# An encoder layer on one core: Fourier position transform split by four, with a three-pass projection

## What is computed

```python
def fourier_mix(f):
    """f: (B,S,FOURIER_WIDTH). Real part of 2-D DFT over (positions, group channels)."""
    B, S, _ = f.shape
    u = f.reshape(B, S, N_FOURIER_GROUPS, FOURIER_GROUP_DIM).astype(jnp.float32)   # 4 groups of 128
    re = jnp.fft.fft2(u, axes=(1, 3), norm="ortho").real
    return re.reshape(B, S, FOURIER_WIDTH).astype(f.dtype)

def encoder_layer(x, ...):
    h = rmsnorm(x, norm1_g)
    q, k, v, f, ga, gf = jnp.split(h @ w_in, SPLITS, axis=-1)
    ...
    o_na = neighborhood_attention(q, k, v, rpb) @ w_na_out
    o_f = fourier_mix(f) @ w_fourier
    x = x + (jax.nn.sigmoid(ga) * o_na + jax.nn.sigmoid(gf) * o_f) @ w_out
    return x + expert_choice_ffn(rmsnorm(x, norm2_g), ...)       # 16 experts
```

## Time and profile before

| | |
|---|---|
| Time, median of 3 runs (lowest to highest) | 2915.61 us (2912.18 to 2917.41) |
| Profiled execution: span from first to last instruction | 2913.2 us |
| Busy: PE, PEld, DVE, ACT, POOL | 91%, 75%, 58%, 42%, 31% |
| Mean granted TensorE clock | 0.956 |
| Tokens, to the first projection | 0 to 32.5 us |
| Fourier, to the last copy to ofT | 32.5 to 245.2 us |

### The profile page before, as it was taken

How to read it: one execution, slowest core, us unless ns; L and a number is a source line. 1 busy time by engine, 2 the same in 40 slices (tenths; PEclk the granted TensorE clock), 3 DMA queues, 4 the chain that set the end, 5 groups by cost and what they waited for, 6 DMA issues and landing times.

```text
span 2913.2 us, 46659 instructions
## 1 busy us (share of the span) xinstructions
PE 2660.3 (91%) x17898; PEld 2197.9 (75%) x17898; DVE 1681.9 (58%) x2075; ACT 1229.0 (42%) x1685; POOL 903.3 (31%) x352
## 2 busy tenths in 40 slices
PE   7999999999999999479989899998999999899997
PEld 4456677676777768368888888888888888888887
DVE  3011422432110143677987887797788779778876
ACT  2011333332000021145665565566566556656554
POOL 0004111110111000234344444434444443443443
PEclk9999999999999999789999999999999999999999
DMA  7211010010110143347787787778778777877872
GB/s 234 40 27 40 17 34 21 6 36 4 40 43 22 29 178 125 144 149 255 266 269 250 258 265 250 258 269 266 249 257 278 250 249 269 268 253 252 287 249 68
DMA packets 340356, 489.78 MB, mean 168 GB/s; under 512 B 22090, under 2 KB 194777, under 8 KB 340192
## 3 DMA queue, kind: packets, MB, share of 16 engines
q1 hardware_dynamic: 332864, 461.60, 46.9%
q0 software_dynamic: 7328, 25.58, 4.1%
HBM read 462.28 MB, written 24.87 MB: 167 GB/s over the span
## 4 chain that ended last, share of the span: by engine, by line
PE 62%; issue 23%; DVE 11%; ACT 2%; DMA 1%; SPq 0%; DVEq 0%; POOL 0%; ACTq 0%; POOLq 0%
PE ps L1267 28%; PE ps L1524 15%; PE ps L1527 7%; PE ps L1447 4%; PE ps L1372 3%; DVE gu L1200 2%; DVE act_f L1207 2%; PE ps L1385 2%; DVE w_lo L434 1%; DVE act_b L1213 1%; DVE act_hl L1215 1%; ACT w_hi L855 1%; PE ps L1514 1%; PE ps L1332 1%; DMA spos_s_sb<-in_spos_s 1%
## 5 line engine op out<-in xcount | busy, mean ns | idle before, releaser
L434 POOL TENSOR_TENSOR w_lo<-raw,w_hi 128x2048 bf16<-128x2048 f32 x132 | 635.5, 4816 | 800.7 <-ACT w_hi L855 800.7
L1524 PE MATMUL ps<-x_hl,w_hi 128*128 128x320 f32 x4112 | 755.9, 327 | 128.4 <-issue 78.3
L855 ACT ACTIVATE w_hi<-raw 128x2048 fp32r<-128x2048 f32 x388 | 739.2, 1906 | 3.0 <-issue 3.0
L1524 PEld LDWEIGHTS ps<-x_hl,w_hi 128*128 128x128 f32 x4112 | 630.2, 195 | 146.0 <-issue 82.6
L434 DVE TENSOR_TENSOR w_lo<-raw,w_hi 128x2048 bf16<-128x2048 f32 x256 | 624.8, 2441 | 96.0 <-ACT w_hi L855 96.0
L1527 PE MATMUL ps<-x_b,w_lo 128*128 128x160 bf16 x4112 | 382.6, 237 | 0.0
L1524 PE MATMUL ps<-act_hl,w_hi 128*128 128x320 f32 x2048 | 349.0, 322 | 0.0
L1527 PEld LDWEIGHTS ps<-x_b,w_lo 128*128 128x128 bf16 x4112 | 279.0, 100 | 54.0 <-issue 3.2
L1524 PEld LDWEIGHTS ps<-act_hl,w_hi 128*128 128x128 f32 x2048 | 311.9, 194 | 2.0
L1207 DVE TENSOR_TENSOR act_f<-silu,gu 128x160 f32<-128x160 f32 x256 | 213.7, 835 | 19.4 <-ACT silu L880 19.4
L873 ACT ACTIVATE lows<-ps 128x320 f32<-128x320 f32 x256 | 111.0, 434 | 254.9 <-PE ps L1527 253.7
(11 more groups left out here) (179 smaller groups left out, 2997.0 us busy)
## 6 DMA issues: line engine op xcount, KB each, us to landing
raw<-in_w_g SPq DMA_DIRECT2D x64, 2048.0 KB, 9.0
raw<-in_w_u SPq DMA_DIRECT2D x64, 2048.0 KB, 11.4
raw<-in_w_d SPq DMA_DIRECT2D x64, 2048.0 KB, 9.1
m_raw<-in_w_in SPq DMA_DIRECT2D x16, 512.0 KB, 4.7
h_raw<-in_w_in SPq DMA_DIRECT2D x12, 512.0 KB, 4.0
x_in<-in_x SPq DMA_DIRECT2D x10, 512.0 KB, 4.2
x_res<-in_x SPq DMA_DIRECT2D x10, 512.0 KB, 4.1
y_out<-x SPq DMA_DIRECT2D x10, 512.0 KB, 2.9
```

Of the source, the lines that this page charges most:

```text
L434: engine.tensor_tensor(unit(w_lo, v), raw_half(v), unit(w_hi, v).bitcast(F32), ALU.subtract)\
L855: act.activation(unit(w_hi, w), raw_half(w), ACT.Copy).then_inc(hi_ready, 1)
L1524: pe.matmul(out, unit(w_hi, v)[:, k, cols], hl[:, k, :, :].rearrange("p a n -> p (a n)"), start=k == 0, stop=False)
```

## The change

**Projection.** The tokens' high and low parts are made tile by tile in the token stage: after each gain ScalarE copies the high part (token_high), GpSimd subtracts for the low one. Each group's weight is split likewise (f_weight_high on ScalarE, then GpSimd), in two buffers, and TensorE projects in three passes, 24 fp32r matmuls for a chunk. The late splits go.

**Positions.** With positions taken modulo four (modulo two for the sample), the transform of 1024 positions becomes four of 256: ScalarE copies tile pairs 0 and 1 (kept), VectorE forms their sums and differences with pairs 2 and 3 in PSUM and then the four turned combinations, TensorE multiplies each by a quarter of the table's rows and columns. The tables are loaded by their first 256 rows (128 for the sample) and regrouped by VectorE, once, so that columns of one remainder lie together. ScalarE writes the result to ofT, at every fourth place (every second for the sample).

**Order.** TensorE runs the channel transform of group g, then the projection of group g+1, then the positions of group g. PSUM banks are assigned anew. The loops over tiles and groups are written out. SP issues the tables without a wait, and each f_w once the one before has been split. GpSimd stores the skewed table and loads the mask after all its token and weight subtractions.

The diff without its memory layout, semaphores and most removed lines:

```diff
+            for u in range(2):
+                sp.dma_start(pos_raw[u][:, :, :], (pos_c, pos_s)[u][0:2 * P, :].rearrange("(k p) n -> p k n", p=P))\
+                  .then_inc(f_tables, 16)
+                sp.dma_start(spos_raw[u][:, :], (spos_c, spos_s)[u][0:P, :]).then_inc(f_tables, 16)
+            for g in range(1, FG):
+                sp.wait_ge(f_w_split, g)
+                f_load(g)
...
+            for t in range(NT):
+                c, first = place_of_tile(t)
+                pool.wait_ge(a_high, t + 1)
+                pool.tensor_tensor(hx_lo[:, :, P * t:P * t + P], hT[:, :, P * t:P * t + P],
+                                   hx_hi[c][:, :, first:first + P].bitcast(F32), ALU.subtract).then_inc(a_split, 1)
+            for g in range(FG):
+                pool.wait_ge(f_w_high, g + 1)
+                pool.tensor_tensor(f_w_lo[g % 2][:, :, :], f_w[:, :, :], f_w_hi[g % 2][:, :, :].bitcast(F32),
+                                   ALU.subtract).then_inc(f_w_split, 1)
             pool.dma_start(skew, rpb_pad[:, :].rearrange("q (o x) -> q o x", o=1)
                            .broadcast_to([HEADS * RPB_H, GRID, SKEW])).then_inc(skew_stored, 16)
             pool.dma_start(mask_sb[:, :], col_mask).then_inc(mask_loaded, 16)
             pool.wait_ge(mask_loaded, 16)
...
+            def token_high(t):
+                c, first = place_of_tile(t)
+                act.wait_ge(a_out, t + 1)
+                act.activation(hx_hi[c][:, :, first:first + P], hT[:, :, P * t:P * t + P], ACT.Copy)\
+                   .then_inc(a_high, 1)
+            def f_weight_high(g):
+                act.wait_ge(f_loaded, 16 * g + 16)
+                if g == 1:
+                    act.wait_ge(a_tr, NT)
+                if g >= 2:
+                    act.wait_ge(f_proj, 3 * (g - 2) + 3)
+                act.activation(f_w_hi[g % 2][:, :, :], f_w[:, :, :], ACT.Copy).then_inc(f_w_high, 1)
+            for t in range(NT):
+                u = t % A_TILES
+                act.wait_ge(a_loaded[u], t // A_TILES * 16 + 16)
+                act.activation(junk_a[:, :], x_in[u][:, :], ACT.Square, accum_out=ss[:, u:u + 1])\
+                   .then_inc(a_stat, 1)
+                inv_rms(a_stat, t * 3, ss[:, u:u + 1], u, D)
+                if t >= 2:
+                    token_high(t - 2)
+            for t in (NT - 2, NT - 1):
+                token_high(t)
+            f_weight_high(0)
+            for g in range(FG):
                 for c, (c0, cn) in enumerate(CHUNKS):
                     act.wait_ge(f_proj, g * 3 + (c + 1))
                     act.activation(fT[:, c0:c0 + cn], bank(c, cn), ACT.Copy).then_inc(f_copied, 1)
+                if g + 1 < FG:
+                    f_weight_high(g + 1)
+                if g:
+                    act.wait_ge(f_mixed, 12 * g)
+                for u in range(2):
+                    act.wait_ge(f_chan, g * 5 + (u + 1))
+                    act.activation(f_kept[u][:, :, :], bank(3 + u).rearrange("p (t n) -> p t n", n=2 * FD),
+                                   ACT.Copy).then_inc(f_copy, 1)
+                act.wait_ge(f_chan, g * 5 + 5)
+                act.activation(fs_kept[:, :], bank(7, 2 * FD), ACT.Copy).then_inc(f_copy, 1)
+                of_s = ofT[:, g, S_PROMPT:TOK].rearrange("p (b a) -> p a b", a=2)
+                of_p = ofT[:, g, 0:S_PROMPT].rearrange("p (b h a) -> p a h b", h=2, a=2)
+                for n, b in enumerate((7, 5, 6)):
+                    act.wait_ge(f_pos, 3 * g + (n + 1))
+                    act.activation(of_p[:, n - 1, :, :] if n else of_s,
+                                   bank(b, BANK if n else S_SAMPLE).rearrange("p (a b) -> p a b", a=2), ACT.Copy)\
+                       .then_inc(f_out, 1)
...
+            def norm(t):
+                u = t % A_TILES
+                dve.wait_ge(a_stat, 3 * t + 3)
+                if t >= 3:
+                    dve.wait_ge(a_tr, t - 2)
+                dve.tensor_scalar(xn_a[t % 3][:, :], x_in[u][:, :], rstd[:, u:u + 1], None, ALU.mult)\
+                   .then_inc(a_norm, 1)
+            def gain(t):
+                dve.wait_ge(a_tr, t + 1)
+                times_gain(hT[:, :, P * t:P * t + P], ps[:, 1024 * (t % 3):1024 * (t % 3) + 1024]
+                           .rearrange("p (k n) -> p k n", n=P), g1_sb[:, :], P).then_inc(a_out, 1)
+            norm(0)
+            for t in range(1, NT):
+                norm(t)
+                gain(t - 1)
+            gain(NT - 1)
+            dve.wait_ge(f_tables, 16 * 4)
+            for u in range(2):
+                dve.tensor_copy(spos_sb[u][:, :, :], spos_raw[u][:, :].rearrange("p (b a) -> p a b", a=2))\
+                   .then_inc(f_regrouped, 1)
+                for n in range(2):
+                    dve.tensor_copy(pos_sb[u][:, n, :, :], pos_raw[u][:, n, :].rearrange("p (b a) -> p a b", a=4))\
+                       .then_inc(f_regrouped, 1)
+            for g in range(FG):
+                done = 12 * g
+                add, sub = ALU.add, ALU.subtract
+                of_bank = [bank(3 + u).rearrange("p (t n) -> p t n", n=2 * FD) for u in range(2)]
+                for u in range(2):
+                    dve.wait_ge(f_copy, 3 * g + (u + 1))
+                    dve.wait_ge(f_chan, 5 * g + (u + 3))
+                    if g:
+                        dve.wait_ge(f_mixed, done)
+                    dve.tensor_tensor(f_sum[u][:, :, :], f_kept[u][:, :, :], of_bank[u], add).then_inc(f_mixed, 1)
+                    dve.tensor_tensor(f_dif[u][:, :, :], f_kept[u][:, :, :], of_bank[u], sub).then_inc(f_mixed, 1)
+                dve.wait_ge(f_copy, 3 * g + 3)
+                if g:
+                    dve.wait_ge(f_pos, 3 * g)
+                for k, op in enumerate((add, sub)):
+                    dve.tensor_tensor(fs_turned[:, k, :], fs_kept[:, :], bank(7, 2 * FD, first=2 * FD), op)\
                        .then_inc(f_mixed, 1)
+                dve.wait_ge(f_mixed, done + 4)
+                for k, op in ((0, add), (2, sub)):
+                    dve.tensor_tensor(f_turned[:, k, :, :], f_sum[0][:, :, :], f_sum[1][:, :, :], op)\
+                       .then_inc(f_mixed, 1)
+                cos, sin = slice(0, FD), slice(FD, 2 * FD)
+                for k, (op_cos, op_sin) in ((1, (sub, add)), (3, (add, sub))):
+                    dve.tensor_tensor(f_turned[:, k, :, cos], f_dif[0][:, :, cos], f_dif[1][:, :, sin], op_cos)\
+                       .then_inc(f_mixed, 1)
+                    dve.tensor_tensor(f_turned[:, k, :, sin], f_dif[0][:, :, sin], f_dif[1][:, :, cos], op_sin)\
+                       .then_inc(f_mixed, 1)
...
+            def tokens_by(weights, c):
+                c0, cn = CHUNKS[c]
+                high, low = hx_hi[c][:, :, :], hx_lo[:, :, c0:c0 + cn]
+                w_hi_, w_lo_ = weights
+                return ([(w_hi_[:, k, :], high[:, k, :]) for k in range(KT)]
+                        + [(w_hi_[:, k, :], low[:, k, :]) for k in range(KT)]
+                        + [(w_lo_[:, k, :], high[:, k, :]) for k in range(KT)])
+            def f_project(g):
+                pe.wait_ge(f_w_split, g + 1)
                 for c, (c0, cn) in enumerate(CHUNKS):
+                    if g == 0:
+                        pe.wait_ge(a_split, (c0 + cn) // P)
+                        if c == 0:
+                            pe.wait_ge(a_out, NT)
+                    product(bank(c, cn), tokens_by((f_w_hi[g % 2], f_w_lo[g % 2]), c)).then_inc(f_proj, 1)
+            def f_channels(g):
                 for pair in range(NT // 2):
                     pe.wait_ge(f_copied, g * 3 + (pair // 2 + 1))
+                    if g and pair == 0:
+                        pe.wait_ge(f_mixed, 12 * g)
+                    if pair in (2, 3):
+                        pe.wait_ge(f_copy, 3 * g + (pair - 1))
+                    if g and pair == 4:
+                        pe.wait_ge(f_out, 3 * g - 2)
+                    b = (3, 4, 3, 4, 7)[pair]
                     for t in (2 * pair, 2 * pair + 1):
+                        op = pe.matmul(bank(b, 2 * FD, first=2 * FD * (t % 2)),
                                        fT[:, P * t:P * t + P], dft_sb[:, :], start=True, stop=True)
                     op.then_inc(f_chan, 1)
+            def f_positions(g):
+                pe.wait_ge(f_mixed, 12 * g + 6)
+                for k in range(2):
+                    op = product(bank(7, P, first=P * k),
+                                 [(fs_turned[:, k, FD * half:FD * half + FD], spos_sb[half][:, k, :])
+                                  for half in range(2)])
+                op.then_inc(f_pos, 1)
+                for n in range(2):
+                    pe.wait_ge(f_mixed, 12 * g + (8, 12)[n])
+                    if g:
+                        pe.wait_ge(f_out, 3 * g - 1 + n)
+                    for h in range(2):
+                        k = n + 2 * h
+                        op = product(bank(5 + n, 2 * P, first=2 * P * h),
```

(80 more changed lines are left out.)

102 lines of the change are left out of this document (37 added, 65 removed).

## The result

| | before | after |
|---|---|---|
| Time, median | 2916.51 us | 2796.49 us (2795.32 to 2798.75, 4 runs) |
| Ratio, 95% interval | | 0.9587 (0.9574 to 0.9601) |
| Span of the profiled execution | 2913.2 us | 2795.7 us |
| Start of the first projection | 32.54 us | 44.73 us |
| Last eviction of ofT ends | 245.17 us | 161.03 us |

The gain is 120 us where the forecast was 77.5, and the time lies under the range. The three moments of the table tell where to look: the Fourier stage ends 84.1 us earlier, the experts begin 78.7 us earlier, and the span is 117.5 us shorter. So 38.8 us of the gain arise in the expert loop, which the change does not touch.

The account below looks back on a forecast made before the run. It took a chain of waits as the bound: token stage to 32.5 us, then TensorE. Start, projections, channel transforms, positions and tail made 167.7 us against 245.17, 77.5 us earlier: 2915.6 - 77.5 = 2838 us, range 2828 to 2853.

Parts of the forecast that it names:

- the sentence on which the sum rests: At the Fourier stage's end: the last ofT eviction's shift, 77.5 us earlier, is the change of the whole span.
- Projection and positions, groups 0 to 2: TensorE, each Fourier group: three-pass projection 13.8 us, 3.6 less; positions split by four 7.95 us, 21 less.
- Group 3's transform and tail: Last Fourier group: channel transform 6.35 us, then 10.7 us for exposed sums, two halves of positions and an eviction.
- The start: Token stage: GpSimd's subtractions and VectorE's normalise ops take turns, so the first projection starts at 49 us.
- ScalarE sets the pace: Token stage: if VectorE's collisions cost nothing, the first projection starts at 44.5 us, total 2833; outside the forecast range 0.09.
- The clock: TensorE: half clock adds 3.0 us to the first projection, nothing between groups; other end 5 to 9 us.
- rival (d): Fourier stage on TensorE: clock stays at 0.50 throughout because of gaps, giving 2941 us; chance 0.02.
- Rival (e): Position matmuls on TensorE: half the columns cost 0.86 us as at 512, 27.7 us return, 2866; chance 0.03.
- 1.5 us for fT: At a group's end TensorE waits for ScalarE's last eviction and first fT chunk: 0.2 + 0.60 + 0.60 and a signal.
- The 0.75 us for the first kept copy: In the channel transform, TensorE's third pair waits 0.75 us more for ScalarE's copy, queued behind fT chunks and weight.
- Strides: ScalarE's stepped ofT writes: exposed evictions cost 0 to 2.4 us, regrouping reads some 1.5; taken as 0.
- Rival (c): Before the heads: GpSimd arrives late, waiting for the mask; a store 10 us slower costs 6 us, 2844; chance 0.07.

Follow-up runs that it names:

- the changed kernel with 144 more: The changed kernel with 144 already satisfied wait instructions added on TensorE ahead of its expert loop: 2839.37 us, ratio 0.9743.
- both in seven blocks: The kernel before with 128 already satisfied waits added on TensorE ahead of its expert loop, 2881.56 us, set against the changed kernel, 2796.49 us.
- with 64 more: The kernel before with 64 already satisfied wait instructions added on TensorE ahead of its expert loop: 3017.84 us, ratio 1.0348.

## Why the prediction was wrong

**What failed** is the sentence on which the sum rests: that the shift of the last eviction of ofT is the change of the span, because what follows keeps its order and its work. It keeps both, but not its place in TensorE's instruction stream. The page of before showed the gap and I did not ask about it: 153 instruction packets, and one TensorE idle time of some 5 us without a releaser per expert. None of the rivals was about the code. With the place held equal the forecast stands close: the changed kernel with 144 more, in eight blocks with one gap as the kernel before, takes 2839.37 us, 6.9 of them for the waits, so 2832.5 us or a gain of 84.0. And both in seven blocks: 2881.56 - 5.0 for the waits, against 2796.49, a gain of 80.1. The rest, some 36 to 40 us, belongs to the place. That the gains come out this near to the forecast's 77.5 us is partly luck: ofT itself ended 84.1 us earlier, 6.7 more than forecast, and in the profiled execution 5.4 us of it were lost behind the stage, within the spread of the attention stage.

**The Fourier stage**, by the terms of the sum, predicted and measured:

| term | predicted us | measured us |
|---|---|---|
| Start of the first projection | 49.0 | 44.73 |
| First projection with the cold clock | 16.8 | 15.91 |
| Channel transform, group 0 | 5.4 | 4.8 |
| Projection and positions, groups 0 to 2 | 3 x 21.75 | 3 x 21.6 |
| Channel transform, groups 1 and 2 | 2 x 7.1 | 2 x 6.67 |
| Group 3's transform and tail | 17.05 | 17.4 |
| Last eviction of ofT | 167.7 | 161.03 |

- **The start** is 4.3 of the 6.7 us. The collision was there: a normalise op takes 1.69 us in place of 0.75 beside GpSimd's subtraction. But a tile does not take the 3.15 us of a subtraction and a whole normalise op in turn. It takes 2.77 us, and the three engines keep step:

```profile
14.99 26.54 POOL L634 TENSOR_TENSOR hx_lo<-hT,hx_hi 128x1024 fp32r<-128x1024 f32 x10 [12.15 <-ACT hx_hi L784]
...
26.73 0.30 ACT L775 ACTIVATE lnv<-ss,eps 128x1 f32<-128x1 f32 x1
27.06 0.20 ACT L778 ACTIVATE rstd<-lnv 128x1 f32<-128x1 f32 x1
27.30 1.69 DVE L997 TENSOR_SCALAR xn_a<-x_in,rstd 128x1024 f32<-128x1024 f32 x1
27.39 1.06 ACT L784 ACTIVATE hx_hi<-hT 128x1024 fp32r<-128x1024 f32 x1
28.35 1.04 ACT L798 ACTIVATE junk_a<-x_in 128x1024 f32<-128x1024 f32 x1
28.91 1.21 DVE L980 TENSOR_TENSOR hT<-ps,g_sb 128x1024 f32<-128x1024 f32 x1
```

  ScalarE's five ops fill a tile but for 0.11 us, in which it waits for the gain; VectorE, with the longer normalise op, has no idle time from 17.81 to 35.66 us; a subtraction takes 2.70 us in place of 2.38, with 0.08 us between two. Which of them sets the pace no run separates. Ten subtractions so took 26.54 us where the sum had 24.0 + 5.2, and the first started at 14.99 us where it had 16.2. The weight's low part took 3.18 us and not 2.4, and the table copies did not delay it. The prediction had a case near this (ScalarE sets the pace, start at 44.5 us) and took the other. That its number is nearer is partly luck, since it had the collisions cost nothing. The step that failed was to add a whole normalise op to each subtraction: the turn costs what it adds to the tile's pace, and ScalarE needs nearly that long anyway.
- **The clock.** The granted clock was 0.50 (1.2 GHz) already from 20 to 45 us, while TensorE had only the transposes and then 8.17 us of idling, and in the first 3.27 us of the projection; the first projection so takes 15.91 us in place of 13.8, a loss of 2.1 where 3.0 was taken from the heads. Between the groups it stayed at 1.00, as forecast. The ground given against rival (d) does not hold throughout, though: in the trace of before the clock was 0.50 from 412 to 422.3 us, with TensorE busy without a break, and not for 7 us at most. Stretch and its length, PE busy, clock, DMA share, GB/s:

```profile
44.73:48.00 3.27, 3.27 (x8) 0.50 0.57 158
48.00:60.40 12.40, 12.40 (x66) 0.97 0.01 2
65.45:79.00 13.55, 13.55 (x72) 1.00 0.14 40
79.05:87.00 7.95, 7.95 (x42) 1.00 0.00 0
```

- **Projection and positions** were right: 13.55 us and 7.95 us, at clock 1.00, where 13.8 and 7.95 stood. Rival (e), half the columns at the old price, is out.
- **The waits in the groups.** 1.5 us for fT was 1.58, for a reason half wrong: the eviction takes not 0.60 but 1.07 us, and the fT chunk behind it adds 0.43 more and not 0.60 (145.14 - 144.71). The 0.75 us for the first kept copy was 0.28: in the chain the weight's high part stands with 0.48 us, not with 1.06.
- **Strides.** Taken as nothing, within 0 to 2.4 us; they cost 1.35 us by one execution each. What the Trainium skill, SBUF — State Buffer, section "Door 1: The DMA port swizzle (why `[64,N]` ≈ `[32,N]`)", says of 16-byte lines, and what was cited against the change, was right in kind: a 512-column eviction with steps of 16 bytes takes 1.07 us in place of 0.60.
- **Rival (c)**, GpSimd late for the heads, did not come: it waits for ofT and not for the mask, and splits the weight 0.16 us behind the eviction.

## What to carry to other kernels

Look at the instruction queue and at idle time without a releaser in a long loop before an edit, and again after it: here a loop of 1642 instructions changed its period by 2.6 to 9% (99.84, 102.44 and, with 64 more, 108.92 us) when code ahead of it grew by 64 or 128 instructions, and 32 were enough to bring the gaps back. Compare two versions with the loop at the same place in its blocks, or the place is taken for the edit. And price a collision by the slack of the op that waits: an op that gets twice as long costs little where another engine needs nearly as long for the same tile.

## What the runs showed of the hardware

- TensorE's loop of 1642 instructions ran without any fetch where it touched seven blocks of 256, and was fetched whole (9 packets of 16 KB) in each round where it touched eight, by the count above: 2799.86 against 2839.37 us for 32 instructions of difference. The fetch behind the branch cost TensorE 4.4 to 5.8 us, 4.9 to 5.2 on the mean of a kernel, that of the second block up to 5.0 more.
- A satisfied wait instruction on TensorE is not free: 128 cost 5.0 us and 192 cost 12.0 us beyond the 8.3 us that TensorE idled there. With 112, 128, 144 and 192 of them the idle time was 11.70, 13.29, 15.23 and 20.40 us, some 0.105 us for each.
- ScalarE writing SBUF in steps of four fp32 needs 1.07 us for 512 columns from PSUM, 0.60 us contiguous; the sample's 256 columns in steps of two need 0.41 against 0.38 us.
- The attention stage's length differs between executions of the same instructions: 445.1 to 449.9 us to the first gate in three of them.
